# The last mixer of a two-block model: narrower output matmuls, one more side step per scan step, a sum in pieces, and gates before GLU

## The reference, cut to what matters

```python
z = h @ w_in
u, qd, fd, idd, gate = jnp.split(z, CD_SPLIT, axis=-1)
yc = s5_mixer(u, ...)            # a diagonal complex scan over time, then GLU
f = lower_bound + (1.0 - lower_bound) * jax.nn.sigmoid(fd)
od = chunked_gated_linear_attention(silu(qd), 1.0 - f, idd, log(f))   # HGRN, 8 heads
yd = head_rmsnorm(od, hgrn_norm_g)
y = jnp.concatenate([yc, yd], axis=-1) * jax.nn.silu(gate)
return y @ w_out
```

## Time and profile before

| | |
|---|---|
| median of 3 runs | 3145.56 us (3145.5 to 3147.03) |
| profiled execution | 3144.75 us, its span in the trace 3143.4 us |
| TensorE matmul busy | 3047.8 us (97%), 26006 records |
| VectorE busy | 2167.4 us (69%) |
| ScalarE busy | 1465.1 us (47%) |
| GpSimd busy | 680.8 us (22%) |
| mean granted TensorE clock | 0.992 |
| moved by DMA | 693.29 MB, mean 221 GB/s |

### The profile page before, as it was taken

The page is one execution under the profiler, slowest core; times in us unless marked ns, Lnnn a source line. Parts: engine busy times, 40 slices in busy tenths (PEclk is TensorE's granted clock), DMA queues, the critical chain, the costliest instruction groups (busy, mean ns, idle before and its releaser), DMA issues. The chain is left out here.

```text
span 3143.4 us, 58119 instructions
## 1 busy us (share of the span) xinstructions
PE 3047.8 (97%) x26006; PEld 2593.7 (83%) x26006; DVE 2167.4 (69%) x2028; ACT 1465.1 (47%) x1418; POOL 680.8 (22%) x753
## 2 busy tenths in 40 slices
PE   8999899999999999999999999999999999999988
PEld 7888788888888888568888888888687878776877
DVE  6777777777757666556767877655776556896655
ACT  4333454545444444564555555434564444212543
POOL 3555144545455200000210000000130000012300
PEclk9999999999999999999999999999999999999999
DMA  9889488888898564544666656754455545554343
GB/s 334 284 311 320 161 283 306 297 299 306 303 325 284 191 206 162 174 159 150 233 230 223 231 206 218 262 201 137 160 175 178 175 172 189 200 211 177 133 150 108
DMA packets 306025, 693.29 MB, mean 221 GB/s; under 512 B 16480, under 2 KB 20704, under 8 KB 299760
## 3 DMA queue, kind: packets, MB, share of 16 engines
q1 hardware_dynamic: 270192, 564.22, 52.1%
q0 software_dynamic: 35584, 125.36, 11.0%
HBM read 625.56 MB, written 63.96 MB: 219 GB/s over the span
## 5 line engine op out<-in xcount | busy, mean ns | idle before, releaser
L645 PE MATMUL PSG<-XH,WS 128*128 128x256 bf16 x11296 | 1846.5, 274 | 24.9 <-DVE WS L1963 7.4
L1746 DVE TENSOR_TENSOR WS<-WF,WS 128x2048 bf16<-128x2048 f32 (+1 forms) x483 | 1190.3, 2486 | 590.9 <-ACT WS L1169 590.3
L645 PE MATMUL PSG<-XL,WS 128*128 128x256 bf16 x5648 | 1490.4, 274 | 1.8 <-DVE XL L1854 1.1
L645 PEld LDWEIGHTS PSG<-XH,WS 128*128 128x128 bf16 x11296 | 1107.6, 98 | 173.6 <-issue 27.2
L1169 ACT ACTIVATE WS<-WF 128x2048 bf16<-128x2048 f32 (+1 forms) x483 | 906.0, 1899 | 632.7 <-PE PSG L645 216.9
L645 PE MATMUL PSG<-SCR,WS 128*128 128x256 bf16 x6720 | 745.5, 273 | 3.6 <-DVE SCR L2315 3.6
L645 PEld LDWEIGHTS PSG<-SCR,WS 128*128 128x128 bf16 x6720 | 659.5, 98 | 86.2 <-issue 4.2
L645 PEld LDWEIGHTS PSG<-XL,WS 128*128 128x128 bf16 x5648 | 554.0, 98 | 71.9 <-DVE XL L1859 2.4
L557 POOL TENSOR_TENSOR SCR<-SCR 128x1024 bf16<-128x1024 f32 x92 | 239.9, 2607 | 5.6 <-DMA weight_halves<-SCR 4.0
L645 PE MATMUL PSG<-WS,XH 128*128 128x512 bf16 x640 | 190.1, 379 | 2.2 <-issue 2.2
L645 PE MATMUL PB<-SCR 128*128 128x128 f32 (+3 forms) x928 | 151.2, 326 | 24.2 <-issue 7.8
(11 more groups left out here) (267 smaller groups left out, 1779.7 us busy)
## 6 DMA issues: line engine op xcount, KB each, us to landing
WF<-ffn_w_up SPq DMA_DIRECT2D x176, 1024.0 KB, 6.5
WF<-ffn_w_down SPq DMA_DIRECT2D x88, 1024.0 KB, 6.4
WF<-ab_w_in SPq DMA_DIRECT2D x56, 1024.0 KB, 5.2
weight_halves<-SCR POOLq DMA_DIRECT2D x184, 256.0 KB, 6.0
WS<-weight_halves SPq DMA_DIRECT2D x46, 1024.0 KB, 4.8
WF<-a_w_in SPq DMA_DIRECT2D x44, 1024.0 KB, 8.9
SCR<-cd_w_in POOLq DMA_DIRECT2D x80, 512.0 KB, 6.9
WF<-a_w_out SPq DMA_DIRECT2D x16, 1024.0 KB, 8.0
```

Source lines behind the costliest of these rows:

```text
L645: return nc.tensor.matmul(o, lhsT, rhs, start=start, stop=stop, skip_group_check=True)
L1746: tt(l, w, h, ALU.subtract).then_inc(s_lo, 1)
```

## The change

Five edits, all in the last mixer:

1. *Own columns per block.* The output matmuls of S5 load only the 32 columns of weights that hold anything, and write their own 32 rows of the bank (each block of 32 is begun and ended by its own two matmuls).
2. *One more side step per scan step.* On TensorE, VectorE and ScalarE 6 side steps lie between scan steps, 7 after odd n. The flow takes 109 steps.
3. *HGRN's running sum in four pieces* of two heads (512 elements a row), on VectorE right behind the scans of steps 9, 11, 13 and 15. Those who read it, or write over what it reads, wait for `s_scan` 5.
4. *S5's gates first, then GLU.* The order is now gates 0 and 1 (S5's two groups), glu, gates 2 and 3 (HGRN's). Both groups of S5 are gated in one flow ahead of gate 3's gemm.
5. *GLU's product a chunk later.* ScalarE makes the sigmoids of a whole gemm into two buffers and frees the bank itself; VectorE multiplies before the steps of the second chunk of the gemm that follows.

```diff
-    for j in (2, 3, 0):
+    for j in (0, 1):
         add("cd_gate", w, 4096 + 512 * j)
     for j in range(2):
         add("glu", A["s5_w_glu"], j * 512)
-    add("cd_gate", w, 4096 + 512)
+    for j in (2, 3):
+        add("cd_gate", w, 4096 + 512 * j)
...
-        SG = STAT[:, 0:2, :]
+        SG = [STAT[:, 0:2, :], SUMS[:, 0:2, :]]
...
-            nc.gpsimd.wait_ge(s_scan, 2)
+            nc.gpsimd.wait_ge(s_scan, 5)
...
-                            last = mm(PB[:, 2, 0:T], CW[:, 640 * r + 128 * q:640 * r + 128 * q + 128], z,
-                                      q == 0 and i == 0, q == 3 and i == 1)
+                            last = mm(PB[32 * q:32 * q + 32, 2, 0:T], CW[:, 640 * r + 160 * q:640 * r + 160 * q + 32],
+                                      z, i == 0, i == 1)
                     last.then_inc(s_yb, 1)
                     if n % 2:
                         bank_free[2] = (s_ty, j + 1)
                         yield
+                    yield
                     yield
...
-            for gi in stage["cd_gate"][0:3]:
+            for gi in stage["cd_gate"][0:2]:
                 gemm(gi, xh, xl, rate=4)
             side.until(s5_flow)
...
-            gated_0 = side.add_first(gated((0,)))
+            gemm(stage["cd_gate"][2], xh, xl, rate=4)
+            gated_s = side.add_first(gated((0, 1)))
             gemm(stage["cd_gate"][3], xh, xl, rate=4)
-            gated_1 = side.add_first(gated((1,)))
...
-                    yield from idle(5 + n % 2)
+                    yield from idle(6 + n % 2)
...
+            for j, gi in enumerate(gates[0:2]):
+                ps = gemm(gi, rate=4)
+                nc.scalar.wait_ge(s_scan, 5)
+                nc.scalar.wait_ge(s_mm, done(gi))
+                act(four(GT1, j), ps[:, :, :], ACT.Silu).then_inc(s_evac[gi % 2], 1)
...
-                for n in range(0, 4, 2):
-                    if 2 * j + n // 2:
-                        nc.scalar.wait_ge(s_glu, 2 * j + n // 2)
-                    for m in range(2):
-                        t = act(SG[:, m, :], ps[:, n + m, :], ACT.Sigmoid, bias=pr("b_glu", 4 * j + n + m))
-                    t.then_inc(s_sg if n == 0 else s_evac[gi % 2], 1)
...
+                if j:
+                    nc.scalar.wait_ge(s_glu, 1)
+                for n in range(4):
+                    t = act(SG[n // 2][:, n % 2, :], ps[:, n, :], ACT.Sigmoid, bias=pr("b_glu", 4 * j + n))
+                t.then_inc(s_evac[gi % 2], 1)
+            keep(gates[2], four(GT1, 2), 4, func=ACT.Silu)
...
+                def scan_piece(p):
+
+                    nc.vector.wait_ge(s_ones, 3)
+                    nc.vector.wait_ge(s_fg, 2)
+                    nc.vector.tensor_tensor_scan(BD[:, 2 * p:2 * p + 2, :].rearrange(flat), ONES[:, 0:512],
+                                                 FF[:, 2 * p:2 * p + 2, :].rearrange(flat), 0.0, ALU.mult,
+                                                 ALU.add).then_inc(s_scan, 1)
...
+                    if n in (9, 11, 13, 15):
+                        scan_piece((n - 9) // 2)
...
-            scan(BD, ONES, FF, 2)
...
+            def gate_u(j):
+
+                nc.vector.wait_ge(*evac(stage["glu"][j]))
+                for n in range(2):
+                    k = 4 * j + 2 * n
+                    t = tt(U[:, k:k + 2, :], U[:, k:k + 2, :], SG[n], ALU.mult)
+                t.then_inc(s_glu, 1)
+
+            glu = stage["glu"]
+            gemm(glu[0], rate=4)
+            gemm(glu[1], rate=4, before=lambda c: gate_u(0) if c == 1 else None)
+            gemm(gates[2], rate=4, before=lambda c: gate_u(1) if c == 1 else None)
+
+            def gated_s5():
+                nc.vector.wait_ge(s_glu, 2)
+                nc.vector.wait_ge(*evac(gates[1]))
+                yield from gated([(5 + g, (four(U, g), four(GT1, g), four(UH, g), four(UL, g))) for g in range(2)])
```

More of the change, by code:

```diff
@@ L271, in two_block_model @@
             sem(n) for n in ("s_bu", "s_br", "s_mg", "s_sscan", "s_xs", "s_yb", "s_ty", "s_uh", "s_ul"))
-        s_gam, s_game, s_fg, s_kd, s_sg, s_glu = (
-            sem(n) for n in ("s_gam", "s_game", "s_fg", "s_kd", "s_sg", "s_glu"))
+        s_gam, s_game, s_fg, s_kd, s_glu = (
+            sem(n) for n in ("s_gam", "s_game", "s_fg", "s_kd", "s_glu"))
         s_xw, s_rr, s_store, s_store_g = sem("s_xw"), sem("s_rr"), sem("s_store"), sem("s_store_g")
@@ L1122, in tensor_program @@
                 gemm(gi, uh, ul, [(s_ul, k // 4 + 1) for k in range(8)] if n == 0 else None, rate=4)
-            gated_0 = side.add_first(gated((0,)))
+            gemm(stage["cd_gate"][2], xh, xl, rate=4)
+            gated_s = side.add_first(gated((0, 1)))
             gemm(stage["cd_gate"][3], xh, xl, rate=4)
-            gated_1 = side.add_first(gated((1,)))
             gated_h = side.add(gated((2, 3)))
             residual("cd_out0", None, uh, ul, [(s_gl, 5 + k // 4) for k in range(8)], rate=4,
-                     before=lambda c: side.until(gated_0, *((gated_1,) if c else ())))
+                     before=lambda c: side.until(gated_s))
             side.until(gated_h)
@@ L1649, in hgrn @@
                     yield
-                nc.scalar.wait_ge(s_scan, 2)
+                nc.scalar.wait_ge(s_scan, 5)
                 nc.scalar.wait_ge(s_ul, 2)
@@ L1670, in scalar_program @@
             gates = stage["cd_gate"]
-            nc.scalar.wait_ge(s_scan, 2)
-            for j, gi in zip(GATE_ORDER[0:3], gates[0:3]):
-                keep(gi, four(GT1, j), 4, func=ACT.Silu)
+            for j, gi in enumerate(gates[0:2]):
+                ps = gemm(gi, rate=4)
+                nc.scalar.wait_ge(s_scan, 5)
+                nc.scalar.wait_ge(s_mm, done(gi))
+                act(four(GT1, j), ps[:, :, :], ACT.Silu).then_inc(s_evac[gi % 2], 1)
             side.until(s5_flow)
@@ L1677, in scalar_program @@
                 nc.scalar.wait_ge(s_mm, done(gi))
-                for n in range(0, 4, 2):
-                    if 2 * j + n // 2:
-                        nc.scalar.wait_ge(s_glu, 2 * j + n // 2)
-                    for m in range(2):
-                        t = act(SG[:, m, :], ps[:, n + m, :], ACT.Sigmoid, bias=pr("b_glu", 4 * j + n + m))
-                    t.then_inc(s_sg if n == 0 else s_evac[gi % 2], 1)
-            def gated_s5(g):
+                if j:
[5 more added lines that the diff above has]
+            def gated_s5():
                 nc.scalar.wait_ge(s_mm, done(stage["glu"][1]))
[L1687 to L1691, removed]
+                yield from gated([(5 + g, (four(U, g), four(UH, g))) for g in range(2)])
+            gated_s = side.add_first(gated_s5())
+            keep(gates[3], four(GT1, 3), 4, func=ACT.Silu)
             def gated_hgrn():
@@ L1697, in scalar_program @@
             gated_h = side.add(gated_hgrn())
-            residual("cd_out0", None, rate=4, before=lambda c: side.until(gated_0, *((gated_1,) if c else ())))
+            residual("cd_out0", None, rate=4, before=lambda c: side.until(gated_s))
             side.until(gated_h)
@@ L2466, in vector_program @@
                 ts(four(KD1, j), four(FF, j), -1.0, 1.0, ALU.mult, ALU.add).then_inc(s_kd, 1)
-            nc.vector.wait_ge(s_ones, 3)
-            nc.vector.wait_ge(s_fg, 2)
-            scan(BD, ONES, FF, 2)
             for gi in stage["qd"] + stage["idd"]:
@@ L2473, in vector_program, with gated_s5 @@
             gates = stage["cd_gate"]
-            for gi in gates[0:3]:
+            for gi in gates[0:2]:
                 gemm(gi, rate=4)
             side.until(s5_flow)
[L2477 to L2492, removed]
+            def gate_u(j):
[8 more added lines that the diff above has]
+            gemm(gates[2], rate=4, before=lambda c: gate_u(1) if c == 1 else None)
+            def gated_s5():
+                nc.vector.wait_ge(s_glu, 2)
+                nc.vector.wait_ge(*evac(gates[1]))
+                yield from gated([(5 + g, (four(U, g), four(GT1, g), four(UH, g), four(UL, g))) for g in range(2)])
+            gated_s = side.add_first(gated_s5())
             gemm(gates[3], rate=4)
-            gated_1 = side.add_first(gated_s5(1))
             def gated_hgrn():
```

## The result

The changed kernel takes **3108.72 us** (median of 4 runs, 3106.28 to 3110.83), the kernel before, beside it, 3146.3: a ratio of 0.988 [0.9868, 0.9892]. That is 1.2% faster, well clear of the noise.

The account below looks back on a forecast made before the run. TensorE, busy 97% of the span, was taken as the bound; 8.2 + 1.6 + 3.9 + 10.0 + 4.0 + 2.0 = 29.7 us off 3144.75 gave 3115.05, forecast as 3116 us (3110 to 3122; wider range 3103 to 3130).

Parts of the forecast that it names:

- slow clock and edges: Behind vanished TensorE waits: 1.6 us of slow clock in the scan, 4.0 in the tail, 2.0 at the waits' edges.
- The output blocks: S5's 16 output blocks: partly overlapping narrow matmuls take 1.49 us a block instead of 1.73, saving 3.9 us.
- rival 2: S5's output blocks overlap fully, as the product does: 10.6 us saved instead of 3.9, 3109 us; chance 0.18.
- Rival 3: Narrow output blocks run serially, waiting for weight loads: 3147 us, or 3165 with full lengths waited out; chance 0.06.
- The extra step: S5's scan: a TensorE pair of 22.6 us gives 2.7 us of slack; waits fall from 13.2 to 5.0 us.
- rival 4: VectorE stays the scan's bound and HGRN later lacks gemm cover; about 8 us gained, 3138 us; chance 0.04.
- HGRN's sum in four pieces: In S5's scan: 0.4 us more on VectorE, within the slack; the wait for ScalarE's logarithm goes.
- The tail's waits: TensorE's waits from the scan's end to 3050 us: 15.0 us less 2.6 and 2.4 left, 10.0 us off.
- Rival 1: The tail's waits come back elsewhere, through S5's gating and GLU's sigmoids: 7.0 us plus 2.8 slow clock, 3126 us; chance 0.17.
- HGRN's start: HGRN's first product behind S5's last output block: between 0 and 5.1 us, taken as 0 with 2.6 in the range.

Follow-up runs that it names:

- e1: The changed kernel with the old wide output matmuls (128 columns, whole bank), other four edits kept: 3117.46 us, mixer 8.1 us more.
- e11: The changed kernel itself, measured again unchanged as a base beside two other runs on the same chip: 3105.03 us.
- e2: The changed kernel, but each output block loads 64 columns, so both blocks of a scan step lie in one 64-column strip: 3121.58 us.
- e4: The changed kernel without the extra side step behind each scan step, other four edits kept: 3129.39 us, mixer 19.7 us more.
- e3: The kernel before with only the narrow output blocks added: 3143.65 us, ratio 0.9992 to the kernel before.
- e5: The changed kernel with HGRN's running sum in one piece at its old place: 3113.69 us, mixer 5.9 us more.
- e9: The changed kernel with S5's two groups gated one chunk later, at gate 3's second chunk: 3105.9 us.
- e7: The changed kernel with S5's second group gated after gate 3, as before the change: 3114.33 us, mixer 4.1 us more.
- e12: The changed kernel with GLU's sigmoids and product done at once, half a bank at a time, new gate order kept: 3117.25 us, mixer 7.2 us more.
- e10: The changed kernel with one more empty side step behind scan step 15, so HGRN's heads start at slot 110, not 109: 3132.55 us.

## Why the prediction was right, step by step

The direction and the range were right, the sum was too small: within the mixer 36.3 us went instead of 29.7; the start 1.0 us later took back one. The 6.6 us more are the blocks (6.2 more), slow clock and edges (1.8 more) and the tail (0.2 more), less the scan's waits (1.6 less). Nearly all is the one term below, whose other bound the range had in it.

- **The output blocks: the term that was mis-sized.** I took 1.49 us a block, "matmuls that start in order, the first of the second block beside the last of the first". Measured: 1.00 us, and about 0.1 at entering (a narrow block starts 0.2 us behind the start of the gemm matmul ahead of it, where the next gemm matmul would start after 0.11): 16 x (1.73 - 1.10) = 10.1 us instead of 3.9. The order of the matmuls, two of one block and then two of the other, did not hinder it: that argument failed, and with it the forecast against rival 2, whose bound of 1.07 is close to what was measured. Undone, it costs 8.1 us (e1; 9.0 beside e11). e2 tells the cause: in one strip the same matmuls take 1.87 us.
- **Rival 3 and the rule on weight loads.** Within a strip the pieces follow each other at 0.216 us, as the wide ones do, with loads of 110 ns among them: but for 0.02 us at the second, no piece waits for its load. The Trainium skill's rule that I weighed ("TensorE: Matmul & The Clock Gate", Part 3: a load overlaps a matmul in flight only where the row groups differ) would have forbidden it, as both blocks use all rows; the trace does not agree for two column strips. Nor does it for the wide blocks before: their loads of 190 ns use all rows too, and the pieces still start every 0.216 us. Rival 3 is out.
- **The extra step.** The pair has 17.0 us of gemm, 2 x 1.07 and, by the measured blocks, 2 x 1.01: 21.2 us instead of 22.6. So the shorter blocks used up the slack, 0.1 us a pair with a piece instead of 1.5, and VectorE takes 21.0 a pair with hardly a gap, where I had named a pair near 22. It held: the scan's waits are 6.6 us where I left 5.0, at the places named (first product 1.2, first outputs 1.05, 2.29 and 0.57, first piece 0.85), with one of 0.38 between that I had not named. That no wait is above 2 us was wrong: the second output's is 2.29, where I had put the mean of 1.0. e4 shows this part carrying 19.7 us, since what it hides grew; e3 shows that the blocks alone give nothing. Of rival 4, VectorE as the bound of the scan holds for e3 and, level with TensorE, almost for the change; its price did not come, since no wait stands where HGRN starts.
- **HGRN's sum in four pieces.** Of what I gave the scan, 4.6 + 1.6 - 1.2 = 5.0 us hung on it (the wait, its slow clock, less the wait left for the first piece); undone it costs 5.9 us (e5).
- **The tail's waits.** 4.8 us left, forecast 5.0: 2.3 on L1529 in five heads (2.6 forecast), and head 5's 2.48 (2.4 forecast, by adding up what ScalarE does behind the gating). e9 shows that this wait comes from where the gating falls, e7 that the join's 3.6 us went because both groups are gated early, e12 that GLU's product at once brings two waits of 3.4 us; of the two "issue" waits before, the longer one had the gating of S5 in it too, as the prediction read it. Rival 1 holds with that one wait only, which the sum had in it.
- **HGRN's start, costed at 0 with 2.6 us in the range.** No wait is listed there in the kernel after. But this was less safe than I made it: e10 moves the heads by one step and loses 24.8 us in the mixer. The prediction named the fall of a head's two products in the chunk as something that wins 1.2 us, and e4, back at slot 96, has that wait again (1.2 us on L2221). At slot 110 it is another wait, that for the weighting, and the place costs twenty times as much; the prediction had no term for it. With four steps a chunk, slots 96 and 109 (remainders 0 and 1) leave the weighting covered, slot 110 (remainder 2) does not; the other remainder was not tried.
- **Slow clock and edges.** 36.3 - 6.6 (scan) - 10.1 (blocks) - 10.2 (tail) = 9.4 us are left for what I had at 1.6 + 4.0 + 2.0 = 7.6. From 2984 us on the clock over 66 us is 0.97 where it was 0.92. I did not divide this remainder further, and no run isolates the 2.0 us of edges.

## What to carry to other kernels

Where two engines are level in a stage, a saving on one of them alone is paid out as waiting (blocks alone: 0 us; with the extra step: 8 us), so look for the pair, and count how much of the new slack the next edit uses up. When several flows are interleaved by a fixed number of steps, the phase in which a long flow starts is a parameter of its own: one empty step cost 27 us here, so each edit that changes a count of steps wants the neighbours tried too. What holds an engine in the middle of a chain (a product that waits for an evacuation) belongs a chunk later, where its input is already there.

## What the runs showed of the hardware

- Two f32 matmul streams in different strips of 32 columns of the array, both with all 128 rows, run fully beside each other although they are issued two and two: eight pieces of 256 columns in 1.00 us, against 1.73 us with 128 columns and 1.87 us in one strip of 64. The two streams start 0.013 us apart. Entering such a block from a full-width gemm matmul of 512 columns takes 0.31 us where the next gemm matmul starts after 0.216.
- Behind the one wait of 2.5 us the clock was granted at 0.83 over 10 us, a mix of 2.4 and 1.2 GHz, and 16 matmuls took 3.30 us; behind the 5.0 us of e5 it was 0.61 over 6 us. The shorter wait does not always bring it: e11, the same kernel, and e1 have the wait of 2.47 us with the clock at 1.00. In e9, where the wait is absent, the 10 us show 1.00 too.
- The place where the last mixer starts varies by 9 us between executions of like kernels. Most of the difference between two executions of the changed kernel arose in the first 300 us (the first f32 matmul starts at 299.3 us in the first one and at 295.5 in e11, the first product of the last mixer at 2688.9 and 2683.9). Differences of 2 us are seen only in the stage itself.
